# A recurrent block and a grid-attention block on one core: half of the value projection moved behind the query projection

## The reference, cut to what matters

```
xn = rms_norm(x) * (1 + scale) + shift          # 512 x 1024
cn = rms_norm(ctx) * (1 + scale_c) + shift_c    # 256 x 1024
f_in, f_gate, q, k, v, na_gate = split(xn @ w_in)     # six parts of 512 columns
kc, vc                         = parts of cn @ w_in
q, k, kc = rms_norm per head of 64, times a gain
f_out  = fourier(f_in) @ w_four * silu(f_gate)
na_out = softmax([q k^T + bias (window of 8 x 16), q kc^T]) [v; vc] * silu(na_gate)
out    = x + gate * (concat(f_out, na_out) @ w_out)
```

## Time and profile before

| | |
|---|---|
| median of 3 runs | 870.62 us (870.25 to 1116.45) |
| the profiled execution, its own time | 871.78 us |
| its span, first to last instruction | 870.0 us |
| mean granted TensorE clock | 0.937 of full speed |
| TensorE busy | 780.4 us, 90% of the span |
| VectorE busy | 501.7 us, 58% |
| ScalarE busy | 301.4 us, 35% |
| GpSimd busy | 210.3 us, 24% |

### The profile page before, as it was taken

How to read it: one execution, slowest core, us unless ns; L and a number is a source line. 1 busy time by engine, 2 the same in 40 slices (tenths; PEclk the granted TensorE clock), 3 DMA queues, 4 the chain that set the end, 5 groups by cost and what they waited for, 6 DMA issues and landing times.

```text
span 870.0 us, 17431 instructions
## 1 busy us (share of the span) xinstructions
PE 780.4 (90%) x7500; PEld 630.8 (73%) x7500; DVE 501.7 (58%) x800; ACT 301.4 (35%) x627; POOL 210.3 (24%) x163
## 2 busy tenths in 40 slices
PE   2599999799699699888877989999997999998997
PEld 2188777677588578777775878888775777776697
DVE  3983898888958413345563321550897566664701
ACT  6334532455422112232334024712334443433300
POOL 0164430455633201222221000290000000000652
PEclk9799999899899658989898999999998999999999
DMA  7023233223355745421003040700320211122221
GB/s 230 24 73 97 76 108 107 73 73 81 79 109 144 147 147 166 135 93 52 3 3 124 24 145 1 187 25 25 88 82 26 73 49 49 50 86 65 81 98 49
DMA packets 116621, 72.82 MB, mean 84 GB/s; under 512 B 26816, under 2 KB 113984, under 8 KB 116544
## 3 DMA queue, kind: packets, MB, share of 16 engines
q1 hardware_dynamic: 81856, 64.07, 24.4%
q10 hardware_dynamic: 34688, 7.62, 4.4%
HBM read 64.35 MB, written 7.34 MB: 82 GB/s over the span
## 4 chain that ended last, share of the span: by engine, by line
PE 76%; DVE 13%; issue 3%; ACT 3%; DMA 2%; ACTq 1%; POOL 1%; POOLq 0%; DVEq 0%
PE bank L515 18%; PE bank L944 8%; PE bank L509 6%; PE bank L510 5%; PE bank L511 5%; DVE arena L1488 3%; PE bank L626 2%; PE bank L672 2%; PE bank L968 2%; PE bank L981 2%; PE bank L751 2%; DVE arena L1586 2%; PE bank L658 2%; PE bank L1063 1%; PE bank L1065 1%
## 5 line engine op out<-in xcount | busy, mean ns | idle before, releaser
L515 PE MATMUL bank<-arena 128*128 128x256 f32 (+1 forms) x768 | 184.6, 400 | 4.5 <-DVE arena L1638 3.1
L515 PEld LDWEIGHTS bank<-arena 128*128 128x128 f32 x768 | 148.3, 196 | 38.5 <-issue 15.4
L1902 POOL TENSOR_TENSOR w_lo<-arena,w_hi 128x1024 fp32r<-128x1024 f32 x24 | 62.8, 2618 | 110.3 <-ACT w_hi L1131 110.3
L509 PE MATMUL bank<-x_hi,w_hi 128*128 128x512 f32 x192 | 80.5, 419 | 4.9 <-DVE x_lo L1494 4.9
L511 PE MATMUL bank<-x_hi,w_lo 128*128 128x512 f32 x192 | 77.1, 402 | 0.0
L1131 ACT ACTIVATE w_hi<-arena 128x1024 fp32r<-128x1024 f32 x44 | 46.5, 1057 | 88.1 <-DMA arena<-w_in 86.7
L510 PE MATMUL bank<-x_lo,w_hi 128*128 128x512 f32 x192 | 77.0, 401 | 0.0
L2005 POOL COPY arena<-arena 128x512 f32<-128x512 f32 x4 | 2.5, 612 | 197.0 <-DVE arena L1812 197.0
L509 PEld LDWEIGHTS bank<-x_hi,w_hi 128*128 128x128 f32 x192 | 37.1, 193 | 15.8 <-issue 7.7
L1586 DVE TENSOR_TENSOR arena<-bank,arena 128x512 f32<-128x512 f32 x32 | 20.6, 686 | 47.3 <-PE bank L626 47.3
L510 PEld LDWEIGHTS bank<-x_lo,w_hi 128*128 128x128 f32 x192 | 37.2, 194 | 10.1 <-issue 1.7
(11 more groups left out here) (245 smaller groups left out, 1698.2 us busy)
## 6 DMA issues: line engine op xcount, KB each, us to landing
arena<-w_in SPq DMA_DIRECT2D x45, 512.0 KB, 3.9
arena<-w_ada SPq DMA_DIRECT2D x12, 1024.0 KB, 5.3
arena<-w_in SPq DMA_DIRECT2D x8, 1024.0 KB, 5.7
arena<-w_out SPq DMA_DIRECT2D x8, 1024.0 KB, 5.1
lt_dram<-arena ACTq DMA_DIRECT2D x16, 256.0 KB, 2.3
arena<-x SPq DMA_DIRECT2D x4, 512.0 KB, 7.5
arena<-x SPq DMA_DIRECT2D x1, 2048.0 KB, 7.7
out<-arena SPq DMA_DIRECT2D x8, 256.0 KB, 2.1
```

What stands on the lines that cost most here:

```text
L509: mm(o[:, :], w_hi[:, wk], x_hi, start=(k == 0), stop=False)
L515: last = mm(o, lhs(k), rhs(k), start=(k == 0), stop=(k == n - 1))
L1902: TT(WLO[n % 3][:, :], WR[n % 3][:, 0:1024], WHI[n % 3][:, :].bitcast(f32), SUB)\
```

## The change

The value projection becomes a function of its half. The first half stays ahead of the keys; the second is called behind the last block of queries. Its weight entry moves from place 47 of the list to place 55, and the entries between (four blocks of keys, four of queries) come one place earlier. The sum of squares of item 11 now stands behind the first bank of that half. ACT copies the second half behind the root of item 11, that is behind all steps of `ITEMS`. The wait for all six banks of values moves from the start of attention to the first product with the values, in step p = 2. `SPLIT_D` names the same 20 blocks in the same order, at their new places.

```diff
-        stream += [cols(w_in2, a + 256 * b, 256) for a in (1536, 2048) for b in range(2)]
+        stream += [cols(w_in2, a, 256) for a in (1536, 1536 + 256, 2048)]
         split_d = len(stream)
-        stream += [cols(w_in2, a + P * b, P) for a in (1536, 1024, 2560, 512, 0) for b in range(4)]
+        stream += [cols(w_in2, a + P * b, P) for a in (1536, 1024) for b in range(4)]
+        stream += [cols(w_in2, 2048 + 256, 256)]
+        stream += [cols(w_in2, a + P * b, P) for a in (2560, 512, 0) for b in range(4)]
...
-        SPLIT_D = list(range(split_d, split_d + 20))
+        SPLIT_D = list(range(split_d, split_d + 8)) + list(range(split_d + 9, split_d + 21))
...
-            for nb in range(2):
+            def project_v(nb):
                 w = weights()
                 for b3 in range(3):
...
                     full(last, ("vv", nb, b3))
+                    if nb and b3 == 0:
+                        head_norm(len(items) - 1)
+
+            project_v(0)
             for name in ("kk", "q"):
                 for c in range(4):
                     qk_output(name, c, None, None)
-            head_norm(len(items) - 1)
+            project_v(1)
...
                 qt, c = divmod(p, NAH // 2)
+                if p == 0:
+                    for nb in range(2):
+                        for b3 in range(3):
+                            stored(pe, ("vv", nb, b3))
...
-            for nb in range(2):
-                for b3 in range(3):
-                    stored(pe, ("vv", nb, b3))
             for p in range(PU + 2):
...
-            def take_v():
-                for nb in range(2):
+            def take_v(nb):
...
-                    take_v()
+                    take_v(0)
...
             root(len(ITEMS) - 1)
+            take_v(1)
```

More of the change, by code:

```diff
@@ L1365, in root @@
                        scale=1.0 if q else 1.0 / HD), ("ss", i))
-            def take_v():
-                for nb in range(2):
[L1369 to L1379, removed]
+            def take_v(nb):
+                at = slice(nb * 256, (nb + 1) * 256)
+                for b3 in range(3):
+                    o = arrived(act, ("vv", nb, b3)).rearrange("p (i n) -> p i n", i=2)
+                    if b3 < 2:
+                        t = V_TILES[2 * b3]
+                        ins = A(VP[:, t:V_TILES[2 * b3 + 1] + 1:b3 + 1, at], o, ACT.Copy)
+                    else:
+                        A(VP[:, 6, at], o[:, 0, :], ACT.Copy)
+                        for h, t in ((0, 4), (1, 0)):
+                            ins = A(VP[side[h], t, at], o[side[h], 1, :], ACT.Copy)
+                    free(ins, ("vv", nb, b3))
             def round_xn():
```

## The result

| | before | changed |
|---|---|---|
| median of 6 runs | 870.43 us (866.97 to 1116.45) | 860.63 us (859.81 to 865.03) |
| profiled execution, its time / span | 871.78 / 870.0 us | 862.83 / 861.0 us |
| ratio, with its 95% interval | | 0.9904 (0.9874 to 0.9934) |

The forecast was 862.3 us. The ratios compare fast runs alone: that leaves out the run of 1116.45 us here, and 11 of before's 23 runs in the round of after_third and gate_sums_early_3 (those of 871 us and more), whose two ratios come out high by it.

What follows compares the result with a forecast made beforehand. TensorE was taken as bound by a late norm chain's wait before attention's second step and the low clock behind it. Gap 6.0 (0.2 from sums included) plus clock 2.3 gave 8.3 us: median 862.3 us, range 860.5 to 866.

Steps and rivals of the forecast that it cites:

- What bounds: Start of attention: TensorE, otherwise full, idles on DVE's late norm chain (661.2 to 667 us), then runs at low clock.
- The gap: TensorE's wait ahead of attention's second-step scores goes whole, from 667.01 to 661.0: 6.0 us gained.
- parted sums: The last two sums of squares, parted by values, cost 1.4 to 1.9 us instead of 1.91: 0.2 us gain.
- The clock: Attention's second step keeps full clock with no gap ahead: 6.49 us instead of 8.79, a gain of 2.3 us.
- DVE: DVE's last norms, covered by the moved values, finish at 648.5 us, 7 us before the first scores.
- the ring: Gate-block loads for steps 10 and 11 are released one product later, landing 3.8 us behind; costed at nothing.
- the table load: ACT's exponential table load now follows the last value copies, ending at 657.95; 1.28 us long, costed at 0.1 us.
- slack of 0.8 us: Attention's second step: banks come free at 660.1, TensorE arrives at 661.0; slack 0.9 us, later given as 0.8.
- Later steps: From attention's second step on only the wait for the values changed; nothing else is late next.
- short wait: Rival: table load or late squares hold TensorE at the second step 0.5 to 3 us; 863 to 866 us, chance 0.13.
- nothing comes of it: Rival: the gap comes back later in attention, or the wait moves to the queries' end; 869 to 872 us, chance 0.06.
- slow rival: Late gate loads hold squares, roots and masks; free up to 12 us landing, 871 to 876 us for 18 to 23; chance 0.04.

Runs made afterwards that it cites:

- after_third: The changed kernel run a third time with no edit; median 861.33 us, ratio to before 0.9946.
- gate_sums_early_3: gate_sums_early with the output product's first bank doing its 24 matmuls that need no late half first; median 860.53 us, ratio to before 0.9925.
- filler_in_gap: The kernel before, plus 22 matmuls that nobody reads behind the gate matmuls of attention's first step; ratio to before 0.9994.
- dve_delay_in_after: The changed kernel, plus four unused reciprocals on DVE between the last head norm and the masks; ratio to before 0.9979.
- gate_rounding_late: The changed kernel, with rounding and splitting of the first two gate blocks moved behind the squares of the last two query blocks; median 860.40 us.
- values_before_last_query: The kernel before, with the values' second half moved ahead of the last query block instead of behind it; ratio to before 0.9994.
- gate_sums_early: The changed kernel, with the two matmuls spreading the output gate moved ahead of the product with w_four; median 858.28 us, ratio to before 0.9906.

## Why the prediction was right, and what it missed

*What bounds.* Right: the gap and the low clock behind it were two prices, and filler_in_gap took the second away alone.

*The gap, 6.0 us.* Measured 6.1: first to second scores 11.27 to 5.46, and 0.3 us from the parted sums (forecast 0.2).

*The clock, 2.3 us.* Measured 2.5 (8.79 to 6.28) at the start of attention. The step without products with the values is 6.28 us and not 6.49.

*DVE, the ring, the table load.* DVE was free 7.8 us ahead of the first scores (7 forecast), the loads landed 3.8 and 3.9 us behind their products, the table load ended 2.45 us after the first scores' start (2.4) and cost nothing. The Trainium skill, "ScalarE: Activation LUTs", section "What ACT_TABLE_LOAD costs", adds 1.38 us of drain to each load. The trace has no room for it on either side: ACT's last copy ends 0.01 us ahead of the load (653.83 + 0.76, and 654.60), and the exponential starts 0.02 us behind its end at 655.88, in a place where it was due, since DVE's mask was done at 655.80. So for this kernel the measurement decides for 1.28 us. The slack of 0.8 us at the second step, worked out from rows, agrees with dve_delay_in_after: 9.03 + 0.8 = 9.8 us free, 13.51 - 3.65 = 9.9 measured.

*Later steps.* Here the prediction failed, though it costs little: "Nothing else is late next" looked for waits and found none, but the clock gave back 1.7 us behind a wait of 1.42 us that both kernels have. So the sum was 8.6 - 1.7 = 6.9 us from mark to end, 0.8% of 870, and not 8.3. That the profiled execution came out at 862.83 us, where 863.5 was worked out, is partly luck: 2.0 us ahead of the mark, which the change doesn't touch, more than made up for the 1.4 us missing behind it. The measured median lay at 9.8 below before. That the 2.9 us beyond the 6.9 are scatter of the same kind is likely and not shown, since only profiled runs have the mark; the three ratios of the changed kernel, 0.9904, 0.9921 and 0.9946, all hold 0.992 in their intervals.

*The rivals.* A short wait was not left. That nothing comes of it fell too: 6.9 us stay to the end of the span. Of the slow rival the runs show only its first part, that the loads have room: with them out of the way (gate_rounding_late) nothing changed. Landings of 12 us were not tried. A wrong step that no number rested on came out in the runs: I took any place behind item 10 for cover of its norm, and values_before_last_query answered with the old wait of 5.74 us.

## What to carry to other kernels

Where a full engine has one gap, put work without a deadline behind the last thing that starts the late chain, and read in the other engines' lists whether the chain can start at all while it runs. A gap on TensorE costs its own length and then the low clock behind it, here 2.5 us for 5.7, 1.6 for 2.7; useless matmuls in the gap win back the second part alone. When runs scatter, find a mark behind the scatter and measure from it: 3 us in 300 showed in single profiles there, and not in medians of up to 12 runs.

## What the runs showed of the hardware

A wait of 1.42 us was enough for the granted clock to fall to 0.50 for about 3 us in five profiles out of eleven, and the wait of 1.41 us that ends 18 us ahead of it never cost anything in fourteen. The Trainium skill, "TensorE: Matmul & The Clock Gate", section "What's actually happening", says that the number of slow matmuls at the start of a kernel changes from run to run. Ahead of the mark the traces agree: in the first 545 us the granted clock was at 0.50 for 106, 96 and 99 us in the three profiles of the changed kernel. At this late place it didn't change: from the start of the product to the output product it is 16.82 us in all three and 15.12 to 15.13 in both of the kernel before, and the other six programs have one of these two values. What fixes it was not found.

A split of 128x512 on DVE took 0.69 us alone and 4.27 beside one of GpSimd's, in the changed kernel:

```profile
802.90 0.69 DVE L1876 TENSOR_TENSOR mix_lo<-arena,mix_hi 128x512 fp32r<-128x512 f32 x1
...
806.33 4.27 DVE L1876 TENSOR_TENSOR mix_lo<-arena,mix_hi 128x512 fp32r<-128x512 f32 x1
```

```profile
805.53 4.52 POOL L2003 TENSOR_TENSOR w_out_lo<-arena,w_out_hi 128x2048 fp32r<-128x2048 f32 x1 [2.61 <-ACT w_out_hi L1446]
```

Behind it DVE's next splits are late as well. TensorE waited 1.41 us for them in gate_sums_early and 0.17 in this kernel and in the one before. The Trainium skill, "SBUF — State Buffer", section "Who interferes with whom", says that a DVE instruction with two inputs from SBUF contends with a GpSimd one that reads SBUF; the trace agrees, with 3.6 us for this one.
